# An mLSTM, cross-attention and SwiGLU block on one core: the first value strip ahead of the query and key strip, with the gate columns inside it

## What is computed

```python
hn = rmsnorm(x, norm_mix)
proj = hn @ a_w_in                         # columns: 1024 qk, 1024 v, 1024 o, 8 gates
qk, v, o, g = split(proj)
qk = silu(causal_dwconv(qk, conv_w))       # four taps along the tokens
g = g + gate_b; i_pre = g[:, :4]; log_f = log_sigmoid(g[:, 4:])
# per head (4), in chunks of tokens, a scan: needs q, k, v, i_pre, log_f of that head
h = scan(q, k, v, i_pre, log_f)
h = head_rmsnorm(h, a_norm) * sigmoid(o)
x = x + h @ a_w_out
# then cross attention on rmsnorm(x), then SwiGLU on rmsnorm(x), then a last rmsnorm
```

## Time and profile before

| | |
|---|---|
| median of 3 runs | 1412.33 us (1408.58 to 1412.37) |
| profiled execution, its own time | 1410.57 us |
| its span | 1408.8 us |
| PE busy | 1374.4 us, 98% of the span |
| DVE, ACT, POOL busy | 943.4, 492.4, 209.0 us |

### The profile page before, as it was taken

The page is one execution under the profiler, slowest core; times in us unless marked ns, Lnnn a source line. Parts: engine busy times, 40 slices in busy tenths (PEclk is TensorE's granted clock), DMA queues, the critical chain, the costliest instruction groups (busy, mean ns, idle before and its releaser), DMA issues.

```text
span 1408.8 us, 18109 instructions
## 1 busy us (share of the span) xinstructions
PE 1374.4 (98%) x6833; PEld 1162.9 (83%) x6833; DVE 943.4 (67%) x1660; ACT 492.4 (35%) x868; POOL 209.0 (15%) x228
## 2 busy tenths in 40 slices
PE   7999999999998999999999999999999998999997
PEld 6988888889888878888877888888888887888887
DVE  5838458458377863554577976677787778877775
ACT  6323213313335453222334533343444434222222
POOL 5001201202303000000005000000000004444441
PEclk9999999999999999999999999999999999999999
DMA  5111201200313220010132132244444449799603
GB/s 181 41 50 31 60 31 31 60 30 31 105 61 107 74 88 32 30 60 7 54 120 105 46 113 98 75 165 159 140 142 164 145 168 366 263 305 316 237 30 120
DMA packets 109255, 156.44 MB, mean 111 GB/s; under 512 B 6448, under 2 KB 67952, under 8 KB 109168
## 3 DMA queue, kind: packets, MB, share of 16 engines
q1 hardware_dynamic: 109168, 155.28, 32.5%
HBM read 112.79 MB, written 42.47 MB: 110 GB/s over the span
## 4 chain that ended last, share of the span: by engine, by line
PE 64%; DVE 3%; issue 1%; ACT 0%; POOLq 0%; POOL 0%; ACTq 0%; DVEq 0%
PE PS L2185 9%; PE PS L2183 9%; PE PS L2184 9%; PE PS L1866 7%; PE PS L1867 6%; PE PS L1868 6%; PE PS L2213 4%; PE PS L2215 4%; PE PS L2214 4%; PE PS L2069 2%; DVE SG L1416 1%; PE PS L2079 0%; DVE xT L1500 0%; PE PS L2247 0%; DVE QK L1449 0%
## 5 line engine op out<-in xcount | busy, mean ns | idle before, releaser
L1866 PE MATMUL PS<-XH,WH 128*128 128x512 f32 (+1 forms) x448 | 174.8, 390 | 3.4 <-issue 3.3
L1868 PE MATMUL PS<-XH,WL 128*128 128x512 f32 (+1 forms) x448 | 168.5, 376 | 0.0
L1867 PE MATMUL PS<-XL,WH 128*128 128x512 f32 (+1 forms) x448 | 168.5, 376 | 0.0
L1500 DVE TENSOR_TENSOR xT<-PS,xT 128x512 f32<-128x512 f32 x128 | 87.6, 688 | 46.9 <-PE PS L1868 46.4
L1708 DVE TENSOR_TENSOR xT<-PS,xT 128x512 f32<-128x512 f32 x120 | 80.8, 688 | 43.2 <-PE PS L2215 42.9
L1866 PE MATMUL PS<-YH,WH 128*128 128x512 f32 x256 | 101.7, 397 | 0.7 <-issue 0.7
L1866 PEld LDWEIGHTS PS<-XH,WH 128*128 128x128 f32 x448 | 84.7, 189 | 19.5 <-issue 4.4
L1868 PE MATMUL PS<-YH,WL 128*128 128x512 f32 x256 | 99.8, 390 | 0.0
L1867 PE MATMUL PS<-YL,WH 128*128 128x512 f32 x256 | 99.7, 390 | 0.0
L1868 PEld LDWEIGHTS PS<-XH,WL 128*128 128x128 f32 x448 | 84.7, 189 | 15.8
L1867 PEld LDWEIGHTS PS<-XL,WH 128*128 128x128 f32 x448 | 84.7, 189 | 14.6
(11 more groups left out here) (386 smaller groups left out, 3467.8 us busy)
## 6 DMA issues: line engine op xcount, KB each, us to landing
forms_hi<-HS SPq DMA_DIRECT2D x56, 256.0 KB, 2.4
raw<-in_f_w_up_dram SPq DMA_DIRECT2D x11, 1024.0 KB, 5.8
rawE<-in_f_w_gate_dram SPq DMA_DIRECT2D x10, 1024.0 KB, 5.7
raw<-in_f_w_down_dram SPq DMA_DIRECT2D x40, 256.0 KB, 3.8
raw<-in_a_w_in_dram SPq DMA_DIRECT2D x8, 1024.0 KB, 5.2
forms_lo<-U SPq DMA_DIRECT2D x32, 256.0 KB, 2.6
XH<-forms_hi SPq DMA_DIRECT2D x16, 512.0 KB, 6.4
XL<-forms_lo SPq DMA_DIRECT2D x12, 512.0 KB, 7.0
```

Source lines behind the costliest of these rows:

```text
L1500: v.tensor_tensor(xt, PS[:, g % NB, :], xt, ALU.add).then_inc(s_fd, 1)
L1866: mm(dst, wh, xh, start=(k == 0), stop=False)
L1867: mm(dst, wh, xl, start=False, stop=False)
L1868: last = mm(dst, wl, xh, start=False, stop=(k == len(tiles) - 1))
```

## The change

The order of the first three strips becomes v, o, qk. The first value strip gets 8 groups of one token tile each, and its weights lie in a new tile `GW` in which 16 more columns follow the 256: the gate weights' high and low parts. So the separate gate product and its transposes go. ACT copies each group out in two activations, values and gate columns (`zg`). The weights of this strip are loaded and split in two halves. Tiles 4 to 7 of x get buffers of their own (`XT4`), ACT copies them out alone, and all low parts of x for c = 0 and 1 are DVE's. The gates' remaining steps stand one to a group in the o strip and at the first group of the qk strip.

```diff
-    STRIPS = [("qk", 0), ("v", 0), ("o", 0)]
+    STRIPS = [("v", 0), ("o", 0), ("qk", 0)]
...
+    GATED = AT["v", 0]
+    ngroups = lambda n: TT if n == GATED else NGROUPS[STRIPS[n][0]]
...
-    for step, (kind, r) in enumerate([("v", 0), ("v", 2), ("v", 3), ("o", 0), ("o", 1), ("o", 3)]):
-        part(kind, 0, r, ("gates", step, None))
+    for step in range(4):
+        part("o", 0, step, ("gates", step, None))
+    part("qk", 0, 0, ("gates", 4, None))
...
-        who = "dve" if c in (2, 3) or (c < 2 and k % 2 == 0) or (c == 5 and k >= KT // 2) else "pool"
+        who = "dve" if c in (2, 3) or c < 2 or (c == 5 and k >= KT // 2) else "pool"
...
+            dst, src = strip_src("v", 0)[0]
+            sp.dma_start(dst[:, 0:KT // 2], src[:, 0:KT // 2]).then_inc(s_w0, 16)
+            sp.dma_start(wg_raw, cols(a_w_in, G0, 2 * H)).then_inc(s_wg, 16)
+            sp.dma_start(dst[:, KT // 2:], src[:, KT // 2:]).then_inc(s_wdma, 16)
+            for t in range(4):
+                sp.wait_ge(s_xin[t], 16)
+                sp.dma_start(xlate[t], x_t[4 + t]).then_inc(s_xin[t], 16)
...
             sumsq(0, 0)
-            split_lo_half(0, 0)
-            pieces(0, range(4))
-            split_lo_half(0, 1)
-            pieces(0, range(4, KT - 1))
+            split_first_half()
             sumsq(0, 1)
-            pieces(0, (KT - 1,))
-            pieces(1, range(KT))
...
+                    if n == GATED:
+                        sc.activation(VV[:, 0, r, 0:DV], bank[:, 0:DV], ACT.Copy)
+                        sc.activation(zg[:, r, :], bank[:, DV:DV + 2 * GCOLS], ACT.Copy).then_inc(s_fa, 1)
...
...
-            split_hi(0)
+            for t in range(4):
+                square_x(t)
+            split_first(0)
             for k in range(KT):
                 pieces(0, (k,))
-                if k in (1, 3, 4, 5):
-                    square_x({1: 4, 3: 5, 4: 6, 5: 7}[k])
-                if k in (1, 3, 4, 5):
-                    half_tile({1: 4, 3: 5, 4: 6, 5: 7}[k])
+                if k == 0:
+                    split_first(1)
+                if 2 <= k <= 5:
+                    late_tile(k + 2)
+                if 1 <= k <= 4:
+                    square_x(k + 3)
             pieces(1, range(KT))
             held = []
             for n in range(NF):
...
+                    if r == 3 and h == 0:
+                        finish_qk(h, 3)
-                elif kind == "v" and r == 0:
+                elif kind == "v" and r == 0 and h:
                     finish_qk(h, 3)
...
+            def first_value(half, between=None):
+
+                wide, narrow = SW + 2 * GCOLS, SW + GCOLS
+                for kk in range(KT):
+                    if between is not None:
+                        between(kk)
+                    lo_ready(pe, half, kk)
+                    for r in range(half * NT, half * NT + NT):
+                        if kk == 0:
+                            wait_bank(GI[GATED, r])
+                        bank = PS[:, GI[GATED, r] % NB, :]
+                        xh, xl = xpart(kk, r * P, P)
+                        mm(bank[:, 0:wide], xh, GW[:, kk, 0:wide], start=(kk == 0), stop=False, skip_group_check=True)
+                        mm(bank[:, 0:narrow], xl, GW[:, kk, 0:narrow], start=False, stop=False, skip_group_check=True)
+                        last = mm(bank[:, 0:SW], xh, col(GATED, kk, 0, SW)[1], start=False, stop=(kk == KT - 1),
+                                  skip_group_check=True)
...
             def late_tiles(kk):
-                if kk in (2, 4):
-                    turn_x(5 + kk // 2)
+                if 1 <= kk <= 4:
+                    turn_x(3 + kk)
                 if kk == 4:
                     wait_strip(0)
                 if kk == 7:
                     spread(0, 1)
 
             pe.wait_ge(s_wl0, 1)
-            two_groups(0, 0, 0, late_tiles)
-            two_groups(0, 1, 1)
+            pe.wait_ge(s_wgs, 1)
+            first_value(0, late_tiles)
+            first_value(1)
```

More of the change, by code:

```diff
@@ L282, in build_block @@
         sqsum = [None, halves(QK[:, 1, 1, :]), SG[:, :, HALF:]]
-        wgp = YH[:, 0, :].rearrange("p (k g) -> p k g", k=KT)
-        grow = VV[0:4 * H, 1].rearrange("p t d -> p (t d)")[:, 0:S]
+        XT4 = sb_at("XT4", [P, 4, S], place["YH"])
+        xlate = [XT4[:, t, :] for t in range(4)]
         fout = xin
@@ L379, in build_block @@
         s_vturn = sem("s_vturn")
-        s_vc = sem("s_vc")
         s_wgs = sem("s_wgs")
@@ L823, in _ @@
                 kind, h = STRIPS[n]
-                for r in range(NGROUPS[kind]):
+                for r in range(ngroups(n)):
                     run_parts(n, r, todo)
@@ L1028, in evac @@
                         act.wait_ge(s_b, TT * (h - 1))
-                    sc.activation(VV[:, h % 2, 2 * r:2 * r + 2, 0:DV], bank.rearrange("p (t d) -> p t d", t=2),
-                                  ACT.Copy).then_inc(s_fa, 1)
+                    if n == GATED:
+                        sc.activation(VV[:, 0, r, 0:DV], bank[:, 0:DV], ACT.Copy)
+                        sc.activation(zg[:, r, :], bank[:, DV:DV + 2 * GCOLS], ACT.Copy).then_inc(s_fa, 1)
+                    else:
+                        sc.activation(VV[:, h % 2, 2 * r:2 * r + 2, 0:DV], bank.rearrange("p (t d) -> p t d", t=2),
+                                      ACT.Copy).then_inc(s_fa, 1)
                 elif kind == "o":
-                    if r == 0 and h == 0:
-                        act.wait_ge(s_gd, 5)
                     if r == 0 and h >= 1:
@@ L1535, in evac @@
                     add_residual(g, r)
-            def out_of_psum(t, k0):
+            for t in range(4):
                 dve.wait_ge(s_turn, t + 1)
-                dst, src = tile_of(t, k0, KT)
+                dst, src = tile_of(t, 0)
                 v.tensor_copy(dst, src).then_inc(s_xt, 1)
-            for t in range(4):
-                out_of_psum(t, 0)
             dve.wait_ge(s_vturn, 1)
[L1546 to L1551, removed]
-            pieces(1, range(KT))
[L1553 to L1557, removed]
+            link(v.tensor_copy(vcols[:, :], PS[:, 0, 0:NVEC]))
+            pieces(0, (0,))
+            pieces(0, (1,))
+            dve.wait_ge(s_wg, 16)
+            link(v.tensor_copy(GW[:, :, SW:SW + GCOLS], wg_raw))
+            v.tensor_tensor(GW[:, :, SW + GCOLS:], wg_raw, GW[:, :, SW:SW + GCOLS].bitcast(F32), ALU.subtract).then_inc(s_wgs, 1)
+            pieces(0, (2,))
+            dve.wait_ge(s_whi, 1)
+            second = slice(KT * P, 2 * KT * P)
+            by_k = lambda t: t.rearrange("p (k n) -> p k n", k=KT // 2)
+            v.tensor_tensor(by_k(WL[:, 0, second]), by_k(raw[:, second]), GW[:, KT // 2:, 0:SW].bitcast(F32),
+                            ALU.subtract).then_inc(s_wlo, 1)
+            pieces(0, range(3, KT))
+            pieces(1, range(KT))
+            dve.wait_ge(s_const, 9)
             lo_ready(dve, 1, KT - 1)
@@ L1933, in two_groups @@
                             last.then_inc(s_mm, 1)
-            def gates(step, b):
[L1936 to L1944, removed]
-                if step == 1:
[L1946 to L1951, removed]
+            def first_value(half, between=None):
[13 more added lines that the diff above has]
+                                  skip_group_check=True)
+                        if kk == KT - 1:
+                            last.then_inc(s_mm, 1)
+            def gates(step, b):
+                if step == 1:
                     pe.wait_ge(s_gd, 2)
```

163 lines of the change are left out of this document (86 added, 77 removed).

## The result

The changed kernel takes 1425.01 us (median of 4 runs, 1424.2 to 1425.43); the kernel before, in 4 runs, 1411.07. The ratio is 1.0096, with a 95% interval of 1.0084 to 1.0109: slower, by 1% or about 14 us. The forecast was 1424.

A forecast was written before the change was run, and what follows sets the result against it. PE's stream was taken as the bound. Work saved (-7.4), the first strip's waits (+11.2), the wait before the first scan (+5.5) and the clock (+3.4) summed to +12.8, 1423.4 to 1425.1; forecast 1424 us, range 1418 to 1430.

The forecast's parts named there:

- The bound: Whole kernel: PE's stream decides, busy 98% of the span; what moves the first scan, at 98.25, moves the end.
- Work saved, -7.4: PE before the first scan: gate product (7.26) and transposes (0.78) go, extra columns cost 0.64; net -7.4 us.
- Start and first half: First value strip, first token half: first matmul at 15.3, second half's `spread` ends at 32.0, first half ends at 33.5.
- The seam: Between token halves: PE waits for ACT to copy group 0, idle from 33.5 to 45.1, 11.6 us instead of 0.84.
- The scan: Ahead of the first scan: PE waits 5.5 us for the convolution, where it waited for nothing before.
- The clock: After each of the two new waits: PE's clock falls to the lower level, 1.7 us each, +3.4 together.
- Case (3): Rival: strip starts at 18.1 (+2.8) or clock stays low twice as long after each gap (+3.4); +16 to +19, chance 0.04.
- the sum of 12.8: All terms to the end: 12.8 us more, from -7.4, +11.2, +5.5 and +3.4; case (1), chance 0.75.
- half of (3)'s excess: The range's upper end, 1430: highest run 1412.4 plus 12.8 plus 4.8 for a late start or longer low clock.
- the one with the clock high (+9.4): Rival: both new waits come, but the clock stays high after them; +9.4 us, chance 0.12.
- the one with a short wait at the seam (+0.1): Rival: between token halves PE goes on at 34.1, as DVE's pieces or ACT's copies come sooner; +0.1, chance 0.06.
- The one on the other side, all waits covered (-7.1, 1403.5): Rival: every new wait is covered and the work saved shows; -7.1, 1403.5 us, chance 0.03.

The follow-up runs named there:

- e8: e3 with the gates' third step moved one group earlier, to qk 3, ahead of the last convolution: 1405.21 us, 0.9953 of the kernel before.
- e10: e8 with three unread float32 matmuls in PE's idle stretch ahead of the strip's first matmul: 1402.22 us, 0.9938 of the kernel before.
- e1: Changed kernel, but ACT copies the first strip's groups 0 to 3 out right after the second half's second high part: 1412.58 us.
- e6: Changed kernel with ACT's copies of groups 0 to 3 ahead of the next strip's high part, behind all high parts of x: 1423.27 us.
- e5: Changed kernel with POOL making the low parts of the odd pieces of x again: 1422.95 us.
- e2: Changed kernel with strips in the order v, qk, o and the gates' steps at qk 0, qk 2, o 0, o 1, o 3: 1420.08 us.
- e3: Changed kernel with both e1's early copies and e2's strip order: 1409.65 us, 0.9991 of the kernel before.
- e4: Changed kernel with unread matmuls filling PE's two idle stretches, 46 at the seam and 24 before the first scan: 1418.91 us.
- e11: The changed kernel, unaltered, profiled once more: 1422.9 us, one run.
- e9: e8 with POOL making the odd low parts of x: 1406.42 us, 0.997 of the kernel before.

## Why the prediction was right

**The bound.** PE's stream decided, as said: the first scan's shift of 10.8 us and the clock's 2.7 behind it came out at the end whole, and the pause at 518 added 1.1.

**Work saved, -7.4.** The strip's matmuls lie at the predicted distances. e8 shows the term: up to the first scan PE is busy 7.4 us less, and the scan starts 6.8 earlier.

**Start and first half.** First matmul at 15.71 for 15.3; `spread` at 31.30 to 31.9 for 32.0; first half's end at 33.4 for 33.5. The chain of ACT through the late tiles was right (high part of block 5 done at 27.45 for 27.7), but that PE's clock mattered there as well only e10 shows. No run gives half of the late tiles' copies back to DVE, so what that part of the change costs is not shown.

**The seam.** Second half at 43.99 for 45.1. DVE's operations came at 0.63 and not at 0.70 apiece, since an operation starts before the one ahead of it is over by its length, and so fourteen of them ended at 41.04 for 41.8. e1 takes out nearly the whole wait, e6 and e5 take out one term each, and the wait shrinks by 9.5, 1.8 and 1.5 us where the sum had 11.0, 1.9 and 2.1 (three low parts of 0.70).

**The scan.** Wait 5.45 for 5.5, start at 109.03 for 109.3. In e2 and e3, with a strip between, it is gone.

**The clock.** Right in kind, e4 shows it by itself, but a single number was taken for what varies: 1.7 twice in the sum, 2.8 and 2.7 in the first profiled execution, 1.8 and 2.2 in e11. The term rested on one row of the start, where the low clock lasted 3.4 us, mostly under work; under work after the new waits it lasted 3.4 to 5.7 us, so 1.7 was the low end. Case (3) had this half, a clock that stays low longer, at 0.04 together with a late start; the start came at 15.71, and the longer clock came in part.

**Luck.** In the first execution 1.1 us more of clock at the seam was cancelled by the seam's wait, which ended 1.1 earlier than the sum had it; the second wait's clock (1.0) and the pause (1.1) were not cancelled. Against the sum of 12.8 the difference of the profiled executions is 14.6, and 12.4 with e11's. The medians differ by 13.9. That the forecast of 1424 lies within about 1 us of 1425.01 and of e11's 1422.9 is in part luck, since the clock alone moves an execution by more than that. The upper bound's "half of (3)'s excess", 4.8, is in fact the middle of that excess (3.2 to 6.2); nothing here hangs on it.

**Cases.** Of the rivals, the one with the clock high (+9.4) is excluded by the windows and by e4, which is what it describes (1.0062, 8.7 us above the kernel before), the one with a short wait at the seam (+0.1) is what e1 built: 1412.58, 1.0012 of the kernel before. The one on the other side, all waits covered (-7.1, 1403.5), is what e8 built: 1405.21.

## What to carry to other kernels

When a strip moves to the front, look at what clears its PSUM banks and where that stands in the clearing engine's own stream: four banks of results waited for an engine that had nine activations ahead of them and was idle between them. A chain of small steps can cost nothing in one place and hold TensorE in another, behind a long step of the same engine, so add up an engine's work behind the last group before a wait, not by strip. Price a long idle stretch of TensorE with the clock as well: behind the wait of 5.4 us another 2.2 to 2.8 were lost here, behind that of 10.6 us 1.7 to 2.8, and matmuls that nobody reads kept the clock up. Profile the same kernel twice before a price of the clock is read from one trace.

## What the runs showed of the hardware

The granted clock falls also after short pauses, and not in each execution: after the pause of 2.06 us it stayed at 1.00 in the kernel before and in one execution of the changed kernel and stood at 0.50 for 3.4 us in the other, with the same instructions around. Of the twelve profiled executions seven have this fall (the changed kernel, e1, e4, e6, e8, e9, e10). Such a fall is worth up to 1.7 us, as much as some edits here. It goes with the spread between runs of one kernel: on one chip the kernel before took from 1407.35 us at a mean granted clock of 0.997 to 1413.31 at 0.992. The Trainium skill (TensorE: Matmul & The Clock Gate, "The HAM clock gate") warns that the point at which the clock changes varies from run to run. The two executions of the changed kernel agree: behind the seam's wait the clock came back at 49.6 in one and at 47.9 in the other, 5.6 and 3.7 us after PE's start.

Plain float32 matmuls with `ident` held the clock as well as those on `fp32r` data: with six records of them between 11.69 and 14.4 the clock was at 1.00 in e10 where it stood at 0.50 in e8. What POOL costs DVE shows in one operation, the first low part of x (128x512, two inputs in SBUF): 0.69 us in e11, 1.08 in the changed kernel and 1.50 in e8, as POOL's write of `WL` ran beside it for 0.14, 0.54 and 0.96 us. The small subtraction for the gate columns (128x64) took 0.23 us in the changed kernel with POOL idle and 1.25 in the kernel before, beside a POOL operation of 1.30. The Trainium skill (GPSIMD Engine Reference, the table's row on SBUF interfaces) says that such operations of DVE contend with POOL; these lengths agree.
